# Splitting the weight tiles of a two-layer diffusion step in pairs

## What is computed

```python
mod = jax.nn.silu(cond) @ w_ada + b_ada                 # shift, scale, gate: 2 conditions
h = rms_norm(x, norm_g) * (1 + scale) + shift
z = h @ w_in                                            # 5632 columns in layer 0, 8192 in layer 1
# layer 0: chunked spatial gating beside grouped-query attention (8 heads)
# layer 1: differential attention (16 heads, two score maps each)
out = mixed @ w_out
x = x + gate * out
```

## Time and profile before

| | |
|---|---|
| median of 3 runs | 2920.69 us (2916.67 to 2921.15) |
| span of the profiled execution | 2917.0 us |
| PE busy | 2717.5 us, 93% |
| DVE busy | 1565.7 us, 54% |
| ACT busy | 1017.8 us, 35% |
| splits, high and low | 944 each, 570.6 and 641.4 us |
| weight transfers | 249.14 MB in queue q1 |

### The profile page before, as it was taken

One profiled execution on the slowest core, in us unless ns is written; L12 is line 12 of the kernel. 1 busy time (PEld: TensorE's weight loads), 2 busy tenths in 40 slices (PEclk: granted clock), 3 DMA queues, 4 the chain that ended last, 5 costly groups with the idle time before them and its releaser, 6 DMA issues.

```text
span 2917.0 us, 40231 instructions
## 1 busy us (share of the span) xinstructions
PE 2717.5 (93%) x12498; PEld 2106.4 (72%) x12498; DVE 1565.7 (54%) x3018; ACT 1017.8 (35%) x2023; POOL 417.3 (14%) x483
## 2 busy tenths in 40 slices
PE   6799999999999899979999999999999999979995
PEld 3488777777777677767877777777777777757774
DVE  5762455555656644446245556655655555555443
ACT  6632343442333334323233333333333333333331
POOL 0000121121122100000121112222211211010001
PEclk9899999999999999989999999999999999979998
DMA  8833444433445545543322222222222222365444
GB/s 322 334 115 112 148 147 141 136 114 129 154 162 171 201 172 181 181 152 119 108 97 82 89 84 78 91 89 88 76 98 75 94 95 88 102 207 191 159 140 176
DMA packets 164952, 400.77 MB, mean 137 GB/s; under 512 B 12936, under 2 KB 14608, under 8 KB 159568
## 3 DMA queue, kind: packets, MB, share of 16 engines
q1 hardware_dynamic: 131104, 249.14, 26.2%
q0 software_dynamic: 33712, 149.96, 14.6%
HBM read 338.24 MB, written 63.18 MB: 138 GB/s over the span
## 4 chain that ended last, share of the span: by engine, by line
PE 74%; DVE 13%; issue 4%; DVEq 4%; ACT 3%; DMA 2%; SPq 0%; ACTq 0%; POOL 0%; POOLq 0%
PE ps L495 55%; PE ps L515 5%; PE ps L382 5%; PE ps L373 3%; DVE w_lo L1032 3%; PE ps L391 3%; DMA w_raw<-in_w_ada_dram 1%; DVE small L914 1%; ACT w_hi L676 1%; DVE work L931 1%; PE ps L474 1%; DVEq L1106 1%; DVE work L1126 1%; PE ps L525 1%; DVE small L835 1%
## 5 line engine op out<-in xcount | busy, mean ns | idle before, releaser
L495 PE MATMUL ps<-w_hi,hT_hi 128*128 128x512 f32 x2800 | 1155.9, 413 | 7.9 <-issue 7.9
L495 PE MATMUL ps<-w_hi,hT_lo 128*128 128x512 f32 x2800 | 1103.6, 394 | 0.0
L495 PE MATMUL ps<-w_lo,hT_hi 128*128 128x512 f32 x2800 | 1100.5, 393 | 0.0
L1032 DVE TENSOR_TENSOR w_lo<-w_raw,w_hi 128x512 fp32r<-128x512 f32 x944 | 641.4, 707 | 683.6 <-ACT w_hi L676 668.0
L676 ACT CAST w_hi<-w_raw 128x512 fp32r<-128x512 f32 x944 | 570.6, 620 | 503.3 <-PE ps L495 452.0
L495 PEld LDWEIGHTS ps<-w_hi,hT_hi 128*128 128x128 f32 x2800 | 531.6, 190 | 136.5 <-issue 42.7
L495 PEld LDWEIGHTS ps<-w_hi,hT_lo 128*128 128x128 f32 x2800 | 529.7, 189 | 117.8
L495 PEld LDWEIGHTS ps<-w_lo,hT_hi 128*128 128x128 f32 x2800 | 532.0, 190 | 89.5
L637 ACT ACTIVATE work<-ps,small 128x640 f32<-128x640 f32 (+1 forms) x192 | 139.1, 725 | 563.8 <-DVE small L917 563.7
L515 PE MATMUL ps<-w_hi,cst 128*128 128x512 f32 x384 | 193.9, 505 | 40.2 <-DVE w_lo L1032 30.4
L914 DVE TENSOR_REDUCE small<-ps 128x1 f32<-128x640 f32 (+1 forms) x200 | 143.7, 718 | 123.4 <-PE ps L382 116.2
(11 more groups left out here) (168 smaller groups left out, 2213.4 us busy)
## 6 DMA issues: line engine op xcount, KB each, us to landing
w_raw<-in_w_in_dram SPq DMA_DIRECT2D x216, 512.0 KB, 3.8
w_raw<-in_w_ada_dram SPq DMA_DIRECT2D x192, 512.0 KB, 4.1
z<-stage POOLq DMA_DIRECT2D x27, 1280.0 KB, 5.4
w_raw<-in_w_out_dram SPq DMA_DIRECT2D x64, 512.0 KB, 5.4
work<-z POOLq DMA_DIRECT2D x72, 320.0 KB, 3.8
work<-in_x_sample_dram POOLq DMA_DIRECT2D x12, 1024.0 KB, 7.1
work<-o POOLq DMA_DIRECT2D x8, 1280.0 KB, 8.2
x<-stage POOLq DMA_DIRECT2D x7, 1280.0 KB, 11.4
```

The lines of the kernel that those rows point to most:

```text
L495: last = nc.tensor.matmul(ps[:, t, :], x[:, kt, t * P:(t + 1) * P], w[:, kt % RING, :], start=(kt == 0 and i == 0), stop=(kt == KT - 1 and ...
L1032: nc.vector.tensor_tensor(w_lo[:, kt % RING, :], w_raw[:, i % RAW, kt % 2, :], w_hi[:, kt % RING, :].bitcast(F32), ALU.subtract).then_inc( ...
```

## The change

`split_hi` and `split_lo` now take two tiles each, kt and kt+1 with kt even, which is one unit of `w_raw` and one half of the ring: one operation of 128x1024 instead of two of 128x512. They are called at every second step only. ACT waits until both tiles that were in that half have been used (`wait_slot_used(act, c, kt + 1)`), DVE until both high parts are there. The semaphores rise by 2. PE's code, the transfers and the sizes of all buffers are the same.

```diff
             def split_hi(c, kt):
                 i = kt // 2
                 act.wait_ge(w_landed[i % RAW], c * 16 * (UNITS // RAW) + 16 * (i // RAW + 1))
-                wait_slot_used(act, c, kt)
-                nc.scalar.copy(w_hi[:, kt % RING, :], w_raw[:, i % RAW, kt % 2, :]).then_inc(w_hi_ready, 1)
+                wait_slot_used(act, c, kt + 1)
+                nc.scalar.copy(w_hi[:, kt % RING:kt % RING + 2, :], w_raw[:, i % RAW, :, :]).then_inc(w_hi_ready, 2)
...
                 for kt in range(KT):
                     k = kt + AHEAD
-                    if k < KT:
+                    if k % 2 == 0 and k < KT:
                         split_hi(c, k)
-                    elif not last:
+                    elif k % 2 == 0 and not last:
                         split_hi(c + 1, k - KT)
...
-            for kt in range(AHEAD):
-                split_hi(0, kt)
+            split_hi(0, 0)
...
             def split_lo(c, kt):
                 i = kt // 2
-                dve.wait_ge(w_hi_ready, c * KT + (kt + 1))
-
-                nc.vector.tensor_tensor(w_lo[:, kt % RING, :], w_raw[:, i % RAW, kt % 2, :],
-                                        w_hi[:, kt % RING, :].bitcast(F32), ALU.subtract).then_inc(w_lo_ready, 1)
+                dve.wait_ge(w_hi_ready, c * KT + (kt + 2))
+
+                nc.vector.tensor_tensor(w_lo[:, kt % RING:kt % RING + 2, :], w_raw[:, i % RAW, :, :],
+                                        w_hi[:, kt % RING:kt % RING + 2, :].bitcast(F32),
+                                        ALU.subtract).then_inc(w_lo_ready, 2)
```

More of the change, by code:

```diff
@@ L1179, in _ @@
             nc.vector.tensor_scalar(gsub[:, :], gsub[:, :], 1.0 - LAMBDA_INIT, None, ALU.mult)
-            for kt in range(AHEAD):
-                split_lo(0, kt)
+            split_lo(0, 0)
             split_chunk(0)
```

## The result

The changed kernel takes **3115.84 us** (median of 4 runs, 3112.63 to 3116.72) against 2920.92 for the kernel before in the same session (4 runs, 2916.67 to 2924.34): a ratio of **1.0665**, 95% interval 1.0649 to 1.068. The forecast was 3079.0 with a range of 2995 to 3140. The profiled execution has a span of 3113.8 us against 2917.0, so 196.8 us are to be found.

The account below looks back on a forecast made before the run. PE was taken to bound projection chunks, VectorE's splits modulation chunks. Terms 34 + 48 + 25 + 7 + 16 + 28 = 158 us on the profiled 2917.0, with the median 3.7 above the span, gave 3079 us, range 2995 to 3140.

Parts of the forecast that it names:

- rival 4: Clock stays at 1.2 GHz through all modulation chunks and heads pay the high end: 3135 us; chance 15%.
- the six behind output projections: Modulation chunks after output projections: 4.1 us more each, 25 us together; 41 if the clock falls there.
- the circle: Round trip of the ring in modulation chunks: 3.6 us for two pairs, 1.8 us a pair against 1.2 before.
- the eight of layer 0: Modulation chunks between layer-0 heads: 15.6 us each in place of 11.7, five with a clock fall; 48 us (31 to 58).
- The first eight: Modulation chunks at the start: 15.0 us each, 17.9 in six with the clock fallen; +34 us (16 to 40).
- I take it that it doesn't before the chunk ends: Modulation chunks: a clock fallen to 1.2 GHz doesn't return before the chunk ends; such a chunk takes about 17.9 us.
- Chunks that build hT: Four chunks where wide splits delay modulation and scalings that PE needs: 2 x 6 + 2 x 1.8 = 16 us (5 to 20).
- Heads: Attention heads: a pair adds 0.96 us to the chain on even tiles; 28 us over all heads (10 to 45).
- 1.9 us a head, 23 us: Layer 1's 12 dense heads: 0.96 at tile 4, some 0.4 from tile 2's pair and 0.5 at tile 10.
- 0.96 passes through in full: Dense heads, tile 4: the transpose already waits 1.17 us for the combination, so the pair's added 0.96 us counts fully.
- a wait of the transposes about doubled: Sign to look for after the change: the transposes' wait for the combination (L930, formerly L931) about doubles.
- Rival 1: Faster through fewer fixed costs: 13 us won in modulation chunks and some 5 in heads, 2902 us; chance 4%.

Follow-up runs that it names:

- kernel 7: The changed kernel with rings of eight tiles, hT_lo cut to two tiles and the third product reading hT_hi: 2971.23 us, ratio 1.0166.
- kernel 8: The changed kernel with ten extra unread 128x192 matmuls behind every second pair in the first eight modulation chunks: 3116.72 us, ratio 1.0668.
- kernel 4: The changed kernel with each pair's split behind the head's steps of the tile in all chunks with heads: 3080.72 us, ratio 1.0556.
- kernel 10: The changed kernel with each pair's split behind the head's steps only in the nine chunks of the dense heads: 3073.12 us, ratio 1.0516.
- kernel 11: The changed kernel with only the pair split at each dense head's tile 2 moved behind the head's steps: 3126.35 us, ratio 1.0713.
- kernel 1: The changed kernel with pairs only in the 24 modulation chunks and narrow splits in the 35 projection chunks: 3035.93 us, ratio 1.0423.

## Why the prediction was right, and where it was not

**The total.** 3116 lies in the range, 37 us above the forecast, and by the number alone rival 4 (3135) is nearer. The trace rules that rival out: the clock did not stay low in all modulation chunks, and the six behind output projections took 91.0 us, not the 101 (60.4 + 41) that it needs.

**Modulation chunks: right.** The wide operations cost 1.22 to 1.25 us on DVE and 1.05 on ACT (1.22 and 1.05 expected), the circle 3.71 us (3.6), a chunk 15.1 us (14.2); of the missing 0.9 us the four circles of a chunk make 0.4, and the rest is its start. The six gave 30.6 us where the term has 25, the eight of layer 0 45.0 where it has 48. In these the clock fell in five, as the forecast says, and those took 17.7 to 18.4 us (17.9 expected), the three others 15.9 to 16.5 (15.6). Here kernel 7 shows the cause, and the reading behind it: before, the circle of 2.2 us for four tiles was hidden under VectorE's 2.4, so the ring didn't show in any wait, and it needed a sum of durations to see how little room it had.

**The first eight: right sum, wrong parts.** 35.6 us against 34, but the step on the clock failed, "I take it that it doesn't before the chunk ends". In most of these chunks it does come back. Stretches of the changed kernel, one after another, all of them inside modulation chunks:

```profile
60.70:64.10 3.40, 1.46 (x5) 0.67 (x4) 2.56 (x3) 2.87 (x3) 0.00 (x0) 1.00 0.70 206
64.10:70.90 6.80, 6.74 (x19) 5.31 (x20) 2.53 (x3) 2.94 (x5) 0.54 (x1) 0.50 0.86 272
70.90:84.60 13.70, 8.66 (x34) 5.08 (x33) 9.17 (x9) 9.49 (x10) 0.53 (x1) 1.00 0.83 287
84.60:88.00 3.40, 3.39 (x8) 2.49 (x8) 1.38 (x3) 1.04 (x1) 0.00 (x0) 0.50 0.94 326
88.00:101.60 13.60, 8.56 (x34) 5.19 (x34) 9.28 (x9) 9.22 (x9) 0.53 (x1) 1.00 0.88 307
```

Behind a stretch in which PE was busy 1.46 of 3.4 us the clock stands at 0.50 (1.2 GHz). There the slower matmuls fill the pauses, PE is busy nearly all the time, and the clock is back at 1.00 (2.4 GHz), where it stays for 13.7 us with PE busy 63% of them. The fall undoes itself here. Not always so soon: in the second chunk the clock stood at 0.50 for 13.7 us, with PE busy 12.3 of them. The six chunks behind it have one fall of 3.4 or 6.8 us each. The seven chunks that can be cut at the next one's start took 16.5 to 18.9 us, where the forecast has 15.0 at the higher level. In kernel 8, where the clock didn't fall, they still took 16.4, and a chunk without a fall in kernel 4 took 15.7. So what the chunks cost at the higher level was set too low (16 us; 28.1 in kernel 8), and the clock too high (18 of the 34 by the forecast; 2 to 8 of the 35.6 by the kernels above). That the excess lies at the chunk starts, with ACT's other work in front of the pair, is the likely reading; no run separates it. Two errors of opposite sign stand behind a good number, and that is luck.

**Not foreseen: a small gain.** The projections behind the six output-side chunks are 4.5 us faster. Before, the clock fell just behind four of these modulation chunks, for 3.4 us of the projection; one of these falls in the kernel before:

```profile
1171.10:1174.50 3.40, 3.40 (x9) 2.63 (x9) 2.79 (x5) 0.62 (x1) 0.00 (x0) 0.50 0.41 152
```

The changed kernel has one such fall. Next to one another, a projection with such a fall takes 58.3 us and one without 56.7, so three falls fewer make 4.8 us. Why they are fewer, no run shows.

**Chunks that build hT: a little low.** 20.9 us against 16, just outside its range of 5 to 20. For F even 8.6 us a chunk where the sum has 6, for F odd 1.9 where it has 1.8; the two tiles behind the scalings got longer by 2.0 and 2.4 us (2.0 each foreseen), the even tiles between by 0.76 (0.5).

**Heads: right place, wrong size.** This is the term that makes the miss: 28 us expected (10 to 45), 58.9 measured; with that in its place the sum would have come out at 3110. The step is "1.9 us a head, 23 us" for the dense ones (44.5 us); the 12 others came to 14.4 us where it has 0.4 each. They cost 3.7 us each: 2.9 us by the median head, tile by tile, the rest by heads in which the clock fell (two falls of 3.4 us in the stretch before; nine, 37.5 us in all, after). By tile of the head, the median time between first matmuls, in us:

| tile | 0 | 2 | 3 | 4 | 5 | 9 | 10 | all 12 |
|---|---|---|---|---|---|---|---|---|
| before | 5.14 | 5.86 | 5.00 | 5.48 | 5.24 | 5.04 | 6.42 | 64.0 |
| after | 5.62 | 6.12 | 6.36 | 5.58 | 5.24 | 5.19 | 6.95 | 66.9 |
| kernel 10 (all pairs late) | 5.14 | 6.13 | 6.32 | 4.00 | 5.24 | 5.04 | 6.42 | 64.1 |
| kernel 11 (one pair late) | 5.62 | 5.86 | 6.34 | 6.40 | 5.75 | 5.19 | 6.95 | 67.9 |

The forecast had 0.96 at tile 4, 0.4 from tile 2 and 0.5 at tile 10. Tile 10 was right (0.53). At tile 3 it saw that the score already waited 0.18 us for the exponential, so had no slack, but charged 0.4 in all; tiles 2 and 3 cost 1.6. It had nothing at tile 0 (0.48). One head in the timeline, the seventh dense one, first before and then after: DVE from the split of tile 2 on, and the score of tile 3. Counted from the head's first matmul, the low splits begin at 11.12 and 12.10 us:

```profile
1889.38 0.69 DVE L1032 TENSOR_TENSOR w_lo<-w_raw,w_hi 128x512 fp32r<-128x512 f32 x1 [0.76 <-ACT w_hi L676]
1890.17 0.82 DVE L914 TENSOR_REDUCE small<-ps 128x1 f32<-128x640 f32 x1
...
1894.26 0.89 DVE L931 SCALAR_TENSOR_TENSOR work<-work,small 128x640 f32<-128x640 f32 x1
1895.24 0.82 DVE L914 TENSOR_REDUCE small<-ps 128x1 f32<-128x640 f32 x1
...
1897.33 0.41 PE L382 MATMUL ps<-kT_hi,qT_hi 64*128 64x320 f32 x1 [0.30 <-ACT work L637]
```

```profile
2041.25 1.23 DVE L1031 TENSOR_TENSOR w_lo<-w_raw,w_hi 128x1024 fp32r<-128x1024 f32 x1 [1.26 <-ACT w_hi L676]
2042.57 0.82 DVE L913 TENSOR_REDUCE small<-ps 128x1 f32<-128x640 f32 x1
...
2045.91 1.81 DVE L930 SCALAR_TENSOR_TENSOR work<-work,small 128x640 f32<-128x640 f32 x1
2047.82 0.82 DVE L913 TENSOR_REDUCE small<-ps 128x1 f32<-128x640 f32 x1
...
2049.91 0.41 PE L382 MATMUL ps<-kT_hi,qT_hi 64*128 64x320 f32 x1 [1.24 <-ACT work L637]
```

Of the 0.98 us by which the low split starts later, 0.48 came from the pair at tile 0 and 0.50 from its own wait for the wide high split (1.26 against 0.76). From there to the combination's end it was 5.77 us and is 6.47: the pair adds 0.54, and the combination takes 1.81 us where it took 0.89, while three short operations ahead of it take 0.76 less. The score's wait goes from 0.30 to 1.24 us. What GpSimd does at that moment, before and after:

```profile
1894.34 1.95 POOL L1358 TENSOR_TENSOR work<-rope_a,work 128x512 f32<-128x512 f32 x1 [0.73 <-issue]
```

```profile
2045.76 1.29 POOL L1357 TENSOR_TENSOR work<-rope_a,work 128x512 f32<-128x512 f32 x1 [0.73 <-issue]
```

Before, the combination began 0.08 us ahead of GpSimd's addition, and the addition was the slow one (1.95 us); after, the addition began 0.15 us ahead, took 1.29, and the combination was the slow one. Whichever of the two starts second is the one that lasts longer. The Trainium skill (SBUF — State Buffer, section "SBUF: two separate sides") has this as a rule: of a VectorE operation with two SBUF inputs and a GpSimd operation that reads SBUF, the first to start keeps the shared port to its end and the other is blocked. The rows agree in the main: the combination ends 0.67 us behind GpSimd's end (2047.05), GpSimd's addition before ended 1.14 us behind the combination's (1895.15), each a little less than the 0.89 and 1.29 us that it takes when it starts first. Over the dense stretch the 48 combinations of this width take either 0.88 to 0.89 us or 1.75 to 2.02, and each of the long ones ends 0.68 us behind the end of a GpSimd operation that had begun between 0.25 us before it and 0.04 us after it. There are 4 long ones before and 12 after: the delayed VectorE work met GpSimd's in another order, and the mean went from 974 to 1141 ns. Kernel 10 has 12 long ones as well and still took only 785.6 us, so a long combination by itself need not cost time.

In all of that stretch PE waited 24.4 us for exponentials (26 times) where it had waited 4.4 (6 times). For the combination, which the forecast watched, it waited 13.1 us where it had waited 16.8: the transposes in tile 4, where "0.96 passes through in full" was expected, moved by 0.1 us only, because the score ahead of them on PE had already taken the delay. The sign that the forecast named, a wait of the transposes about doubled, did not appear.

The same place in kernel 11 shows why moving one pair did not help. DVE, then PE's next tile:

```profile
2051.34 1.88 DVE L1036 TENSOR_TENSOR w_lo<-w_raw,w_hi 128x1024 fp32r<-128x1024 f32 x1 [2.02 <-ACT w_hi L677]
2053.38 0.82 DVE L918 TENSOR_REDUCE small<-ps 128x1 f32<-128x640 f32 x1 [0.16 <-issue]
...
2053.27 0.50 PE L496 MATMUL ps<-w_hi,hT_hi 128*128 128x512 f32 x1 [0.87 <-DVE w_lo L1036]
```

The score in tile 3 waits 0.55 us in place of 1.24 in this head. But the moved pair now ends at 2053.22, and tile 4's first matmul waits 0.87 us for it; tile 3 is no shorter. It also stands ahead of the reduction of the next step, which starts 22.85 us into the head in place of 21.94, and tiles 4 and 5 get longer by 0.82 and 0.51 us. Kernel 10 has that wait for the moved pair too (tile 3 at 6.32), but there the pair at tile 4 no longer stands ahead of the combination, and the transposes' wait is gone: tile 4 takes 4.00 us. So the 44.5 us come back only by way of a wait that the kernel before had as well. That the falls of the clock (nine after, nine in kernel 11, five in kernel 10) follow from these waits fits, but no run separates them, and kernel 1 has six falls there with the splits of the kernel before.

**The chance of a gain: rightly small.** The Trainium skill (VectorE: DVE Perf Modes, section on the TRN2 errata) says that a large tile pays the exposed latency once, and asks for tiles of 512 elements or more. The splits before had 512 columns already; that they should be made wider still is the forecast's reading of it. The traces agree with the page on the price (an estimate of 1.22 us by its formula, 1.22 to 1.25 in the rows), and VectorE's busy time fell by 55 us; as a rule for this kernel's time the reading came out the wrong way. Rival 1 said that its result needs a circle under 2.3 us; it was 3.71, and even with a ring of eight, where the wide splits follow one another every 1.14 us, the chunk took the same 10.1 us.

## What to carry to other kernels

Before operations of a producer are merged, add up the round trip of a buffer in the ring (each engine's time for one hand-over, one after the other) and divide it by the number of hand-overs that the ring holds: four tiles in two pairs are two. A ring whose round trip is just under the busiest engine's time shows no wait in the profile, and has no room to be coarsened. And where an engine serves two chains in order, an operation's cost to the other chain is its length plus its own wait for input; look for the reader that has no slack (here the score, which already waited 0.18 us), and charge the whole delay to it.

## What the hardware showed that was not expected

- The clock's fall ended by itself, after 3.4 or 6.8 us in most of the first eight chunks and after 13.7 us in one: with pauses of 1.4 us in each 3.7 the clock stood at 1.00 for 13.7 us at a time, PE being busy 8.6 to 8.7 us of them, and fell behind longer pauses, most of them near chunk starts.
- An operation of VectorE that started while GpSimd was at work took longer (the 128x640 combination 1.81 in place of 0.89 us, the 128x1024 split 1.88 in place of 1.23), and one of GpSimd that started while VectorE was at work likewise (1.95 in place of 1.29 us). All 16 long combinations of the two dense stretches ended 0.68 us behind GpSimd's end.
- Ten small matmuls behind every second pair raised the granted clock of a stretch from 0.83 to 0.94 and left it 2 to 8 us shorter than in the kernels without them; none of it reached the end of the kernel.
